# A layer norm's sum of squares: one level of adds on VectorE, the last four partial sums added by four accumulating matmuls

## The chip, the cores and the metric

The kernel runs on one core of a Trainium2 chip. The metric is the time of one execution on the device in microseconds (us). "Before" has three timed runs and one profiled run.

## What is computed

The reference is one inference step of a two-layer decoder trunk: 528 prompt rows (512 and 16 meta rows) and 32 decode rows, 1024 channels wide. Each layer has a sparse attention branch and a short-convolution branch, their gated merge, an output projection, a layer norm, a squared-ReLU MLP and a second layer norm. The change lies in the layer norm alone, which occurs twice per layer:

```python
def _layernorm(x, g, b):
    xf = x.astype(jnp.float32)
    mu = jnp.mean(xf, axis=-1, keepdims=True)
    xc = xf - mu
    var = jnp.mean(jnp.square(xc), axis=-1, keepdims=True)
    y = xc * lax.rsqrt(var + LN_EPS) * g.astype(jnp.float32) + b.astype(jnp.float32)
    return y.astype(x.dtype)
...
    x = _layernorm(ALPHA * x + mix, ln1_g, ln1_b)
    hdn = jnp.square(jax.nn.relu(x @ w_up))
    return _layernorm(ALPHA * x + hdn @ w_down, ln2_g, ln2_b)
```

## The kernel before

Activations are kept transposed: tile X has the 1024 channels as 8 chunks of 128 partitions, and the 560 rows lie along the free axis (R = 560). The engines run hand-written programs that meet at semaphores; the order of each engine's work is the order of the code.

**Matrix products.** fp32 accuracy is made of three products of split numbers: each weight column block (1024 by 128) is loaded by DMA into ST (L321, issued by SyncE), ScalarE casts the high part WH (`high`, L949), GpSimd subtracts to get the low part WL (`rest`, L395), and TensorE runs WH, WL with the activations' high part and WH with their low part (`unit`, L504 for all 560 rows; `half_unit` and `products`, L489, for one half of 280 rows). The activation parts are AXh/AXl and AHh/AHl. ST has two buffers; a buffer is loaded again when GpSimd has read it.

**The layer norm in halves.** The rows are normalised in two halves of 280 (RH). With two layers, two norms per layer and two halves there are eight passes, numbered q = 0 to 7. Even q is the first half of a norm, odd q the second. One pass goes through the engines so:

1. VectorE adds each product column block to X (`residual`, L1782 or L1783) and sums the chunks into XS (`xs_add`, L1774 and L1776).
2. TensorE multiplies XS with the tile `ones`, which holds 1/1024 (`half_mean`, L528): every partition of PSUM tile PB then has the mean.
3. VectorE subtracts it from X (`ln_center`, L1423, two instructions of 4 chunks).
4. ScalarE squares into SQ (`ln_squares`, L975, two instructions of 4 chunks): 8 chunks of 280.
5. VectorE adds the 8 chunks of SQ in three levels, 8 to 4 to 2 (L1430, twice), then 2 to 1 into SS (L1431), and raises `ln_red` (`ln_squares_sum`).
6. TensorE waits for `ln_red` and multiplies SS with `ones` (`half_var`, L534).
7. ScalarE takes the root into SD (`ln_root`, L981), VectorE the reciprocal into RSTD (`ln_inverse`, L1436).
8. VectorE scales X chunk by chunk (L1443), ScalarE adds the shift and writes AXh (L988, L989), VectorE writes AXl (L1447), each chunk raising `a_ready` for the next products.

**What stands around the passes.** In the even passes (q = 0, 2, 4, 6) TensorE runs half products of the output or down projection between the mean and the variance (`out_halves(ph, done, 7, 10)`), and the last two (`10, 12`) behind it; then it starts the products of the next stage, which need `a_ready`. VectorE runs `column_halves`: column half 8's residual and XS add stand right behind `ln_squares_sum`, then those of half 9, then the reciprocal, four scalings, half 10, four more scalings, half 11. ScalarE and GpSimd prepare the next weight blocks in between: ScalarE's cast of one block stands right behind `ln_root`. In the odd passes q = 1, 3, 5 TensorE has products of the next stage for the finished first half on both sides of mean and variance (`up_halves` or `p1_half`). Pass q = 7 stands alone at the end: mean, variance, then the transposes for the output.

Before `ln_squares_sum`'s first add and between its instructions VectorE waits for its own previous instruction (`own.link`).

Of the kernel before, what the change touches and what calls it, by code (L numbers as in the profile page):

```python
# [12 lines left out]
F32 = mybir.dt.float32  # L13
# [5 lines left out]
ALU = mybir.AluOpType  # L19
# [3 lines left out]
P = 128  # L23
# [7 lines left out]
R = RP + RS  # L31
RH = R // 2
# [108 lines left out]
def trunk_program(nc, a):  # L141
    with ExitStack() as ctx:

        def sb(name, shape, dt):
            return ctx.enter_context(nc.sbuf_tensor(name, shape, dt))

        def arena(name, nbytes):

            off = (nc.sbuf_base + 31) // 32 * 32
            sb(name, [P, nbytes // 4], F32)  # L150
            return off

        def at(name, shape, dt, off):
            return nc.alloc_sbuf_tensor_at(name, shape, dt, offset=off)
# [11 lines left out]
        off_q = arena("r_q", BIG)  # L166
        Q = at("Q", [P, KC, R], F32, off_q)
        SD = at("SD", [P, R], F32, off_q)
        RSTD = at("RSTD", [P, R], F32, off_q + 4 * R)
        XS, SS = at("XS", [P, R], F32, off_q + 8 * R), at("SS", [P, R], F32, off_q + 12 * R)  # L170
        off_sg = arena("r_sg", BIG)
        SG = at("SG", [P, KC, R], F32, off_sg)
        QI = at("QI", [P, 4, R], F32, off_sg)
# [51 lines left out]
        SQ = at("SQ", [P, KC, RH], F32, off_m)  # L225
# [7 lines left out]
        ones = sb("ones", [P, P], F32)  # L233
# [18 lines left out]
        PB = ctx.enter_context(nc.psum_tensor("PB", [P, 4, 512], F32))  # L252
# [4 lines left out]
        def sem(name):  # L257
            return ctx.enter_context(nc.semaphore(name))
# [38 lines left out]
        xs_ready, ln_red, ln_hi = sem("xs_ready"), sem("ln_red"), sem("ln_hi")  # L297
        ln_sum, ln_dev, ln_sq, ln_var, ln_sd, ln_norm, ln_aff = (sem("ln_sum"), sem("ln_dev"), sem("ln_sq"),
                                                                sem("ln_var"), sem("ln_sd"), sem("ln_norm"), sem("ln_aff"))
# [183 lines left out]
        def _(pe):  # L483
# [47 lines left out]
            def half_var(q):  # L531
                pe.wait_ge(ln_red, q + 1)
                h = q % 2
                pe.matmul(PB[:, 2 * h + 1, 0:RH], ones[:, :], SS[:, RH * h:RH * h + RH], start=True, stop=True  # L534
                          ).then_inc(ln_var, 1)


            pe.wait_ge(const_in, 16 * (NPG + 7 + 10))
# [12 lines left out]
            for l in range(DEPTH):  # L551
# [11 lines left out]
                for i in range(6):  # L563
                    p1_half(i)
                    if l > 0 and i == 0:
                        half_mean(4 * l - 1)
                    if l > 0 and i == 2:
                        half_var(4 * l - 1)
# [41 lines left out]
                for r in range(1, 5):  # L610
                    c0, n = PTILES[r]
                    for h in range(IH):
# [7 lines left out]
                        for k0 in range(0, KW[r], 512):  # L620
                            k1 = min(k0 + 512, KW[r])
                            for i, (x, y) in enumerate(((QIh[h // 2], KDh), (QIl[:, h // 2], KDh), (QIh[h // 2], KDl))):
                                mm = pe.matmul(PS[j % 2][0:n, k0 // 512, 0:k1 - k0], x[hp, c0:c0 + n], y[hp, k0:k1],  # L623
                                               start=(i == 0), stop=(i == 2))
# [23 lines left out]
                for q in range(4):  # L648
# [6 lines left out]
                    for par in range(2):  # L655
                        for j in range(4):
                            mm = pe.matmul(PS[par][32 * j:32 * j + 32, jh, :],
                                           QS[ID * par:ID * par + ID, 4 * g + j].rearrange("p h s -> p (h s)"),
                                           KIT[j][ID * par:ID * par + ID, :], start=True, stop=True)
# [4 lines left out]
                for b in range(NB):  # L664
                    b4 = 32 * (b % 4)
                    mm = pe.matmul(PB[b4:b4 + 32, 0, 32 * (b // 4):32 * (b // 4) + 32],
                                   QS[0:ID, b].rearrange("p h s -> p (h s)"), KD[0:ID, RP:R], start=True, stop=True)
# [4 lines left out]
                for par in range(2):  # L672
                    for jh in range(2):
                        col = 512 * (2 * par + jh)
                        for g in range(2):
                            pe.matmul(PS[par][0:RS, jh, :], WIB[:, g, :], RELU_S[g][:, col:col + 512],
                                      start=(g == 0), stop=(g == 1))
                for g in range(2):
                    mm = pe.matmul(PB[0:RS, 1, 0:RS], WIB[:, g, :], RELU_S[g][:, PAST:KEYS_S],
                                   start=(g == 0), stop=(g == 1))  # L680
# [12 lines left out]
                for n in range(KVH):  # L693
                    apart(pe, started)
                    with pe.Fori(0, GRP) as i:
                        c = i + GRP * n
# [86 lines left out]
                for g in range(2):  # L783
# [19 lines left out]
                    for q in range(8):  # L803
                        c, n = q // KVH, q % KVH
# [4 lines left out]
                        for b4 in range(4):  # L809
                            mm = pe.matmul(PB[32 * b4:32 * b4 + 32, c, :],  # L810
                                           QP[:, 4 * g + b4, n].rearrange("p h s -> p (h s)"), KTR[b4][:, :],
                                           start=(n == 0), stop=False)
                        mm.then_inc(kt_mm, 1)
                        if n == KVH - 1:
                            if g == 0 and c == 0:
# [3 lines left out]
                                      stop=True).then_inc(ls_mm, 1)  # L819
# [24 lines left out]
                    for c in range(5):  # L844
# [3 lines left out]
                        for j in range(w):  # L848
                            for b4 in range(4):
                                if c in (0, 2) and j == 0:  # L850
# [3 lines left out]
                                mm = pe.matmul(out_s[32 * b4:32 * b4 + 32, :], pt, vv,  # L854
                                               start=(c == 0 and j == 0), stop=(c == 4))
# [36 lines left out]
                half_mean(4 * l)  # L892
                out_halves(WO, l * 24, 7, 10)
                half_var(4 * l)
                out_halves(WO, l * 24, 10, 12)
                up_halves(0, 1)
                half_mean(4 * l + 1)
                up_halves(1, 3)
                half_var(4 * l + 1)
                up_halves(3, 12)  # L900
                for s in range(2):
# [477 lines left out]
        def _(dve):  # L1379
            own = Chain(dve, dve_own, started)  # L1380
# [45 lines left out]
            def ln_squares_sum(q):  # L1426
                h = q % 2
                dve.wait_ge(ln_sq, 2 * q + 2)
                for n in (4, 2):
                    own.link(dve.tensor_tensor(SQ[:, 0:n, :], SQ[:, 0:n, :], SQ[:, n:2 * n, :], ALU.add))  # L1430
                dve.tensor_tensor(SS[:, RH * h:RH * h + RH], SQ[:, 0, :], SQ[:, 1, :], ALU.add).then_inc(ln_red, 1)  # L1431

            def ln_inverse(q):
                rows = slice(RH * (q % 2), RH * (q % 2) + RH)
# [15 lines left out]
            for l in range(DEPTH):  # L1450
# [11 lines left out]
                if l > 0:  # L1462
                    q = 4 * l - 1
                    ln_center(q)
                    ln_squares_sum(q)
                    ln_inverse(q)
                    ln_scale(q, 0, KC)
                    own.link(dve.tensor_scalar(IDX[:, :], IDX[:, :], float(n_rows), None, ALU.add))
                    half_rows().then_inc(idx_ready, 1)
# [51 lines left out]
                for r in range(1, 5):  # L1521
                    c0, n = PTILES[r]
# [15 lines left out]
                for r in range(1, 5):  # L1538
                    n = PTILES[r][1]
# [3 lines left out]
                with own.fori(TOPK_P // 8, 8):  # L1543
                    for r in range(1, 5):
                        n = PTILES[r][1]
                        own.wait(behind=3)
                        own.count(dve.max(top[0:n, r - 1, :], TK[r][0:n, :]))
                    for r in range(1, 5):
                        n = PTILES[r][1]
# [5 lines left out]
                for r in range(1, 5):  # L1555
                    n = PTILES[r][1]
# [161 lines left out]
                for g in range(2):  # L1718
                    for t in range(1, 32, 2):
# [6 lines left out]
                        if t in (11, 19, 27):  # L1726
                            c = (t - 11) // 8
# [75 lines left out]
                def column_halves(group, q, scale, ws):  # L1803
                    for i in range(7):
                        column_half(group, i, scale, ws)
                    ln_center(q)
                    column_half(group, 7, scale, ws)
                    ln_squares_sum(q)
                    column_half(group, 8, scale, ws)
                    column_half(group, 9, scale, ws)  # L1810
                    ln_inverse(q)
                    ln_scale(q, 0, 4)
                    column_half(group, 10, scale, ws)
                    ln_scale(q, 4, KC)
                    column_half(group, 11, scale, ws)
# [14 lines left out]
                ln_center(q)  # L1830
                up_half(0)
                ln_squares_sum(q)
                up_half(1)
                up_half(2)
# [93 lines left out]
```

## Time and profile before

| | |
|---|---|
| Median of 3 runs | 2580.15 us (2579.83 to 2580.17) |
| The profiled execution | 2578.84 us, its span 2577.0 us |
| Mean granted clock of TensorE | 0.941 of full speed |
| TensorE matmuls busy | 2317.9 us, 90% of the span |
| VectorE busy | 1498.2 us, 58% |
| ScalarE busy | 795.6 us, 31% |
| GpSimd busy | 791.7 us, 31% |
| Instructions | 45632 |

The profiled execution took 1.31 us less than the median, and its span, from the first to the last instruction, 1.84 us less than the execution. Busy shares are means over stages of different kinds: where TensorE waits for VectorE in one stage, the 90% says nothing about it. Matmuls are pipelined, so a row's duration is longer than the time until the next can start. An fp32 matmul (L528, L534) shows as two rows, called passes below. A bracket at a row's end is the idle time of the engine before it, and what ended it.

### The profile page before, as it was taken

How to read it: one execution, taken by the hardware profiler on the slowest of the kernel's cores; microseconds unless marked ns; L12 is line 12 of the kernel's file. 1: busy time of each engine (PE TensorE's matmuls, PEld its weight loads, DVE VectorE, ACT ScalarE, POOL GpSimd, SP SyncE). 2: the span in 40 equal slices, each digit the busy share in tenths (PEclk: the TensorE clock that was granted, in tenths of full speed). 3: DMA queues.
4: the chain of work that ended last, by engine and by line, in shares of the span. 5: the costliest groups of instructions: out<-in, count | busy, mean ns of one | idle time of the engine just before them, and what ended most of it. 6: DMA issues, size and time to landing. Idle time of an engine off the chain costs nothing.

```text
span 2577.0 us, 45632 instructions
## 1 busy us (share of the span) xinstructions
PE 2317.9 (90%) x17143; PEld 2129.0 (83%) x17159; DVE 1498.2 (58%) x2234; ACT 795.6 (31%) x1379; POOL 791.7 (31%) x384
## 2 busy tenths in 40 slices
PE   5988999998669999999998889999975899999996
PEld 4965988898339899999998489888953698999995
DVE  3759877779556632132585797777855566132145
ACT  2233343331111432232242443333221125222233
POOL 2410322224213423333542022222331242343440
PEclk9977999999879999999999699999997899999998
DMA  4420222225732312323343022222464232223230
GB/s 117 132 61 10 73 59 59 62 57 184 283 131 65 99 57 83 89 82 90 110 128 88 2 65 56 59 57 57 138 226 193 91 99 73 74 81 88 83 98 35
DMA packets 321366, 238.03 MB, mean 92 GB/s; under 512 B 9560, under 2 KB 309576, under 8 KB 313080
## 3 DMA queue, kind: packets, MB, share of 16 engines
q1 hardware_dynamic: 304424, 154.69, 21.6%
q0 software_dynamic: 12032, 77.07, 7.6%
q10 hardware_dynamic: 4816, 4.96, 0.6%
q8 instruction: 67, 1.10, 0.2%
q14 instruction: 27, 0.22, 0.0%
HBM read 231.73 MB, written 4.96 MB: 92 GB/s over the span
## 4 chain that ended last, share of the span: by engine, by line
PE 78%; DVE 11%; ACT 4%; issue 3%; DMA 2%; ACTq 1%; SPq 0%; DVEq 0%; POOL 0%; POOLq 0%
PE PS L504 54%; PE PS L489 8%; PE PS L797 3%; DVE BB L1690 2%; PE PB L714 2%; PE PS L623 2%; PE PB L738 2%; PE PB L810 1%; DVE SG L1690 1%; PE PS L854 1%; DVE SG L1725 1%; DVE SQ L1430 1%; DMA KVB<-in_cache_v_dram,IDXH 1%; DVE TKS L1575 1%; PE PB L726 1%
## 5 line engine op out<-in xcount | busy, mean ns | idle before, releaser
L395 POOL TENSOR_TENSOR WL<-ST,WH 128x1024 fp32r<-128x1024 f32 x290 | 704.8, 2431 | 1526.1 <-ACT WH L949 1526.0
L949 ACT CAST WH<-ST 128x1024 fp32r<-128x1024 f32 x290 | 303.7, 1047 | 1090.3 <-PE PS L504 943.9
L504 PE MATMUL PS<-AXh,WH 128*128 128x280 f32 x2688 | 575.6, 296 | 21.0 <-DVE AXl L1758 12.6
L504 PE MATMUL PS<-AXl,WH 128*128 128x280 f32 x2688 | 571.6, 294 | 0.0
L504 PE MATMUL PS<-AXh,WL 128*128 128x280 f32 x2688 | 566.4, 292 | 0.0
L504 PEld LDWEIGHTS PS<-AXh,WH 128*128 128x128 f32 x2688 | 432.0, 190 | 23.0 <-issue 21.6
L504 PEld LDWEIGHTS PS<-AXl,WH 128*128 128x128 f32 x2688 | 432.8, 191 | 0.0
L504 PEld LDWEIGHTS PS<-AXh,WL 128*128 128x128 f32 x2688 | 428.1, 190 | 0.0
L504 PE MATMUL PS<-AHh,WH 128*128 128x280 f32 x1152 | 242.0, 291 | 3.6 <-DVE AHl L1823 3.4
L504 PE MATMUL PS<-AHl,WH 128*128 128x280 f32 x1152 | 243.1, 292 | 0.0
L504 PE MATMUL PS<-AHh,WL 128*128 128x280 f32 x1152 | 241.0, 290 | 0.0
L1822 DVE TENSOR_TENSOR MT<-MT 128x560 f32<-128x560 f32 (+1 forms) x76 | 96.3, 1267 | 238.0 <-ACT AHh L1317 217.1
L504 PEld LDWEIGHTS PS<-AHh,WH 128*128 128x128 f32 x1152 | 182.9, 188 | 4.7 <-DVE AHl L1823 3.9
L504 PEld LDWEIGHTS PS<-AHl,WH 128*128 128x128 f32 x1152 | 183.7, 189 | 0.0
L504 PEld LDWEIGHTS PS<-AHh,WL 128*128 128x128 f32 x1152 | 181.6, 188 | 0.0
L797 PEld LDWEIGHTS PS<-ident,KVB 128*128 128x128 f32 x512 | 69.5, 166 | 102.7 <-DVE KTR L1723 42.6
L797 PE MATMUL PS<-ident,KVB 128*128 128x128 f32 x512 | 84.8, 323 | 75.4 <-DVE KTR L1723 39.6
L1782 DVE TENSOR_TENSOR X<-X,PS 128x560 f32 (+2 forms) x60 | 37.2, 621 | 195.7 <-PE PS L504 165.4
L1572 DVE MAX8 top<-TKS 32x8 f32<-32x2080 f32 x64 | 147.3, 2302 | 3.2 <-DVE TKS L1575 2.9
L1575 DVE MATCH_REPLACE8 TKS<-top,TKS 32x2080 f32<-32x2080 f32 x64 | 147.0, 2297 | 0.0
L489 PE MATMUL PS<-AXh,WH 128*128 128x280 f32 x384 | 119.1, 310 | 20.3 <-DVE AXl L1447 11.1
L489 PE MATMUL PS<-AHh,WH 128*128 128x280 f32 x384 | 113.6, 296 | 3.8 <-issue 3.8
(249 smaller groups left out, 3459.1 us busy)
## 6 DMA issues: line engine op xcount, KB each, us to landing
ST<-in_w_in_dram SPq DMA_DIRECT2D x114, 512.0 KB, 3.8
ST<-in_w_up_dram SPq DMA_DIRECT2D x64, 512.0 KB, 4.1
ST<-in_w_down_dram SPq DMA_DIRECT2D x64, 512.0 KB, 3.8
ST<-in_w_conv_out_dram SPq DMA_DIRECT2D x16, 512.0 KB, 3.8
ST<-in_w_attn_out_dram SPq DMA_DIRECT2D x16, 512.0 KB, 3.8
ST<-in_w_o_dram SPq DMA_DIRECT2D x16, 512.0 KB, 3.8
NAT<-in_x_prompt_dram SPq DMA_DIRECT2D x4, 512.0 KB, 3.9
o_y_dram<-NAT ACTq DMA_DIRECT2D x4, 512.0 KB, 2.6
```

The source lines that it names most:

```text
L395: pool.tensor_tensor(WL[slot][:, :, :], ST[s][:, :, :], WH[slot][:, :, :].bitcast(F32), ALU.subtract).then_inc(lo_done[s], 1)
L489: mm = pe.matmul(out, x[:, k, :], y[:, k, r0:r1], start=(k == 0 and y is hi and x is WH[slot]), stop=(k == KC - 1 and y is lo))
L504: mm = pe.matmul(out[:, h, 0:RH], x[:, k, :], y[:, k, RH * h:RH * h + RH], start=(k == 0 and y is hi and x is WH[slot]), stop=(k == KC - 1 ...
L623: mm = pe.matmul(PS[j % 2][0:n, k0 // 512, 0:k1 - k0], x[hp, c0:c0 + n], y[hp, k0:k1], start=(i == 0), stop=(i == 2))
L714: mm = pe.matmul(bank, QST[:, c0:c0 + m], KT[:, n, k0:k1], start=False, stop=True)
L738: mm = pe.matmul(PB[:, 3, 0:m], VN[0:k1, kt, HD * n:HD * n + HD], PPT[i % 2][0:k1, m * kt:m * kt + m], start=(kt == 0), stop=(kt == keys(r ...
L797: tr = pe.transpose(banks[t % 3][:, P * j:P * j + P], KVB[c // 2][b4][:, 4 * (c % 2) + j, HD * n:HD * n + HD], ident[:, :])
L949: act.copy(WH[slot][:, :, :], ST[s][:, :, :]).then_inc(hi_done[s], 1)
L1572: own.link(dve.max(top[0:RS, 0, :], TKS[:, :]), alone=True)
L1575: own.link(dve.match_replace(TKS[:, :], top[0:RS, 0, :], TKS[:, :], NEG_TAKEN), alone=True)
L1690: own.link(dve.reciprocal(v, v))
L1822: own.link(dve.tensor_tensor(h, h, h, ALU.mult))
```

## The change

VectorE does only the first of the three levels of adds, from 8 chunks to 4, and raises `ln_red` there. TensorE multiplies each of the four remaining chunks of SQ with `ones` and accumulates in the same PSUM columns. Tile SS is gone. Nothing else is moved: every other instruction keeps its place in its engine's order.

```diff
-        XS, SS = at("XS", [P, R], F32, off_q + 8 * R), at("SS", [P, R], F32, off_q + 12 * R)
+        XS = at("XS", [P, R], F32, off_q + 8 * R)
...
             def half_var(q):
                 pe.wait_ge(ln_red, q + 1)
                 h = q % 2
-                pe.matmul(PB[:, 2 * h + 1, 0:RH], ones[:, :], SS[:, RH * h:RH * h + RH], start=True, stop=True
-                          ).then_inc(ln_var, 1)
+                for c in range(4):
+                    mm = pe.matmul(PB[:, 2 * h + 1, 0:RH], ones[:, :], SQ[:, c, :], start=(c == 0), stop=(c == 3))
+                mm.then_inc(ln_var, 1)
...
             def ln_squares_sum(q):
                 h = q % 2
                 dve.wait_ge(ln_sq, 2 * q + 2)
-                for n in (4, 2):
-                    own.link(dve.tensor_tensor(SQ[:, 0:n, :], SQ[:, 0:n, :], SQ[:, n:2 * n, :], ALU.add))
-                dve.tensor_tensor(SS[:, RH * h:RH * h + RH], SQ[:, 0, :], SQ[:, 1, :], ALU.add).then_inc(ln_red, 1)
+                dve.tensor_tensor(SQ[:, 0:4, :], SQ[:, 0:4, :], SQ[:, 4:8, :], ALU.add).then_inc(ln_red, 1)
```

## Rows read from the trace of the kernel before

**Rows 1.** Page, the chain that ended last: shares of the span.

```profile
PE 78%; DVE 11%; ACT 4%; issue 3%; DMA 2%; ACTq 1%; SPq 0%; DVEq 0%; POOL 0%; POOLq 0%
```

**Rows 2.** Source view of L1431: duration in ns, least/median/most.

```profile
L1431 DVE TENSOR_TENSOR SS<-SQ x8: 449/450/2607, 872.3 to 2554.4; 128x280 f32<-128x280 f32 x8
```

**Rows 3.** Timeline, TensorE at q = 6: start us, us, engine, line, operation.

```profile
2534.79 0.29 PE L489 MATMUL PS<-AHl,WH 128*128 128x280 f32 x1
2534.91 0.63 PE L534 MATMUL PB<-SS,ones 128*128 128x280 f32 x2
...
2535.52 0.29 PE L489 MATMUL PS<-AHh,WL 128*128 128x280 f32 x1
```

**Rows 4.** Timeline, TensorE at q = 1.

```profile
897.17 0.29 PE L489 MATMUL PS<-AXl,WH 128*128 128x280 f32 x1
897.77 0.74 PE L534 MATMUL PB<-SS,ones 128*128 128x280 f32 x2 [0.31 <-DVE SS L1431]
...
898.47 0.28 PE L489 MATMUL PS<-AXh,WL 128*128 128x280 f32 x1
```

**Rows 5.** Timelines of GpSimd, VectorE and TensorE at q = 0.

```profile
872.46 2.57 POOL L395 TENSOR_TENSOR WL<-ST,WH 128x1024 fp32r<-128x1024 f32 x1 [0.77 <-ACT WH L949]
876.96 2.40 POOL L395 TENSOR_TENSOR WL<-ST,WH 128x1024 fp32r<-128x1024 f32 x1 [1.92 <-ACT WH L949]
...
873.17 2.17 DVE L1774 TENSOR_TENSOR XS<-XS,X 128x280 f32<-128x280 f32 x1
...
878.28 1.39 DVE L1443 SCALAR_TENSOR_TENSOR X<-X,PL,RSTD 128x280 f32<-128x280 f32 x1
...
881.27 0.37 PE L489 MATMUL PS<-AXh,WH 128*128 128x280 f32 x1 [1.53 <-DVE AXl L1447]
```

**Rows 6.** Timelines of VectorE, TensorE, ScalarE, GpSimd and SyncE's queue at q = 2.

```profile
1278.62 2.82 DVE L1430 TENSOR_TENSOR SQ<-SQ 128x560 f32<-128x560 f32 x1
1281.47 2.49 DVE L1431 TENSOR_TENSOR SS<-SQ 128x280 f32<-128x280 f32 x1
...
1284.02 0.74 PE L534 MATMUL PB<-SS,ones 128*128 128x280 f32 x2 [1.84 <-DVE SS L1431]
...
1284.79 0.49 ACT L981 ACTIVATE SD<-PB,eps 128x280 f32<-128x280 f32 x1 [3.81 <-PE PB L534]
1285.18 1.04 ACT L949 CAST WH<-ST 128x1024 fp32r<-128x1024 f32 x1
...
1286.30 2.40 POOL L395 TENSOR_TENSOR WL<-ST,WH 128x1024 fp32r<-128x1024 f32 x1 [2.65 <-ACT WH L949]
...
1287.74 1.27 DVE L1443 SCALAR_TENSOR_TENSOR X<-X,PL,RSTD 128x280 f32<-128x280 f32 x1
...
1280.87 0.37 SPq L321 DMA_DIRECT2D ST<-in_w_in_dram  x1
```

**Rows 7.** Page, DMA issues: KB each, median us from issue to landing.

```profile
ST<-in_w_in_dram SPq DMA_DIRECT2D x114, 512.0 KB, 3.8
ST<-in_w_up_dram SPq DMA_DIRECT2D x64, 512.0 KB, 4.1
```

**Rows 8.** Timelines of SyncE's queue and ScalarE at q = 4.

```profile
2124.59 0.37 SPq L321 DMA_DIRECT2D ST<-in_w_up_dram  x1
...
2128.89 1.04 ACT L949 CAST WH<-ST 128x1024 fp32r<-128x1024 f32 x1
```

**Rows 9.** Timelines of VectorE and TensorE from q = 6's reciprocal to q = 7's sum.

```profile
2536.18 1.91 DVE L1436 RECIPROCAL RSTD<-SD 128x280 f32<-128x280 f32 x1
...
2547.20 1.30 PE L528 MATMUL PB<-XS,ones 128*128 128x280 f32 x2 [5.46 <-DVE XS L1776]
...
2553.65 0.74 DVE L1430 TENSOR_TENSOR SQ<-SQ 128x560 f32<-128x560 f32 x1
...
2554.93 1.30 PE L534 MATMUL PB<-SS,ones 128*128 128x280 f32 x2 [6.43 <-DVE SS L1431]
```

**Rows 10.** Windows, at q = 7: engines' busy us (instructions), then granted clock, DMA, GB/s.

```profile
2555.00:2556.00 1.00, 1.00 (x2) 0.66 (x3) 0.00 (x0) 0.00 (x0) 0.00 (x0) 0.50 0.00 0
```

## The prediction, made before the changed kernel was run

> **What bounds the kernel now.** I read the chain that ended last first: 78% of it is TensorE and 11% VectorE [rows 1]. So work added to TensorE costs its full time unless TensorE waits there anyway, and work taken from VectorE is worth only what TensorE, or the last norm, waits for it. The eight norm passes must therefore be read one by one. The timelines show four kinds.
>
> q = 1, 3, 5: TensorE comes to the variance, waits 0.31 us for the last add by the trace's reckoning, and goes on with products without a break [rows 4]; the other two show the same 0.31. TensorE is the path.
>
> q = 0, 2, 4: the reader is to see two things. TensorE waits after the variance for the first scaled chunks (1.53 us at q = 0), so VectorE is the path [rows 5]. And VectorE itself is held by GpSimd: the XS add at 873.17 takes 2.17 us where 0.45 is usual for 280 columns [rows 2, 5]; GpSimd's subtraction ran from 872.46 to 875.03, and the add ended 0.31 us behind it. Two of the instructions that the change removes are stretched so too: 2.82 and 2.49 us at q = 2 [rows 6].
>
> q = 6: GpSimd has no work left, TensorE does not wait at the variance [rows 3], but the chain behind it does wait: TensorE stands idle 5.46 us until the last XS add releases the next mean [rows 9].
>
> q = 7: everything is in series, at half clock [rows 9, 10].
>
> **The price of a pass.** An fp32 matmul is two passes. At q = 6 the matmul rows before and behind are 2534.79 and 2535.52; without the sum two steps of the usual 0.12 to 0.13 us would lie between them, so the two passes took 0.73 - 0.25 = 0.48 us, 0.24 each [rows 3]. Three more matmuls are six more passes: 1.44 us at full clock. Bounds: 0.23 to 0.30 a pass (at q = 1, after a wait, from 897.77 to 898.47 are 0.70 us with one product in it [rows 4]). I take 0.24, the row where the sum follows other matmuls without a stop, as it will.
>
> **q = 1, 3, 5.** The sum could have started one step behind 897.17, at 897.30; it started at 897.77, and the second product behind it at 898.47, so 1.17 us from 897.30. After the change the first add is long done when TensorE comes: 0.61 us (the same stretch at q = 6, from 2534.91 to 2535.52) and 1.44 = 2.05 us [rows 3, 4]. Each costs 2.05 - 1.17 = 0.88 us; three of them **+2.6 us** (bounds 2.4 to 3.7). The root comes as much later, and so does what ScalarE does behind it; VectorE's two saved adds are worth nothing there.
>
> **q = 0.** TensorE does not wait at the variance and needs 1.44 us more behind it, which its 1.53 us idle ahead of 881.27 just covers [rows 5]. VectorE is rid of two adds, but the add of column half 8 then meets the subtraction that stretched them, and the root is 1.44 us later: by the order of the code the reciprocal comes some 0.7 us earlier, and the first scaling could start at about 877.6. GpSimd's next subtraction lasts from 876.96 to 879.36, and before the change the scaling ended 0.31 us behind that end (878.28 + 1.39 = 879.67). It is stretched to the same end: **0** (bounds -1.6, the 0.7 us and the stretch of 1.39 against 0.50 both gained, and +0.3, if TensorE is late).
>
> **q = 2.** Here TensorE waited 1.84 us for the stretched adds [rows 6]. Now it starts its sum at about 1282.1, and the root stands 0.77 + 1.44 us behind that, at 1284.3 instead of 1284.79. The reciprocal takes 1.9 us and the first scaling can start at about 1286.8. The cast behind the root can move up too, to 1284.7, because its weight tile was asked for at 1280.87 and lands 3.8 us later [rows 6, 7]. With it GpSimd's subtraction moves from 1286.30 to about 1285.8, still ahead of the scaling, and ends 0.5 us earlier; the scaling ends 0.3 us behind it. **-0.5 us** (bounds 0 and -1.8: the reciprocal's lead of 1.0 us, from 1287.74 - 1.9 = 1285.8 to 1284.8, and the stretch of 1.27 against 0.50). The other 1.3 us of TensorE's former wait are late somewhere else: TensorE waits for scaled chunks instead.
>
> **q = 4** is the same, except that the tile asked for at 2124.59 lands after 4.1 us, at 2128.69, against a cast at 2128.89: **-0.2 us** [rows 7, 8] (bounds 0 and -1.8, as at q = 2).
>
> **q = 6.** The root comes 1.44 us later, and the reciprocal at 2536.18, which stood right behind it, too; scaling, halves 10 and 11 and the XS add follow in line up to the mean that TensorE waits for [rows 9]: **+1.4 us** (bounds 1.3 to 1.8).
>
> **q = 7.** The second add (0.74) and the last (0.45) with the steps between go: TensorE starts when the second add did, at about 2553.67 instead of 2554.93, 1.26 us earlier [rows 2, 9]. The six passes run at the granted clock of 0.50, the 1.2 GHz level [rows 10]: 0.24 at 2.4 GHz is 0.47 there, 2.8 us. **+1.5 us** (bounds +0.2 and +1.6).
>
> **The sum:** 2.6 + 0 - 0.5 - 0.2 + 1.4 + 1.5 = +4.8 us. The profiled execution took 2578.84 us and would take 2583.6; the median of the runs is 1.31 us above it, so I forecast 2580.15 + 4.8 = **2585.0 us**, 0.19% more. A measurement of this kernel can tell about 0.2%, 5.2 us: a forecast just inside "no difference". That tile SS goes costs and moves nothing.
>
> **Who inherits the stretch.** The rows say that a stretched instruction ends when GpSimd's does, so taking the stretched one away hands the stretch to the next of its kind, here the XS add of column half 8 and later the first scaling [rows 5]. The Trainium skill, "SBUF — State Buffer", section "Who interferes with whom", has this as a rule: a VectorE instruction with two SBUF inputs and a GpSimd instruction that reads SBUF exclude each other for the whole instruction, whichever starts first. By it the gains at q = 0, 2, 4 stay as small as in my sum; reading the stretch as the adds' own gives the "faster" rival below. The trace agrees with the rule in the XS add's 2.17 us.
>
> **Rivals.**
>
> *Slower: GpSimd takes the lead away at q = 2 and 4 too.* If the cast cannot start earlier than before, because the tile lands later than 4.3 us after its request (1280.87 to 1285.18), the subtraction holds the first scaling until the old time, as I already expect at q = 0. The two gains are 0 and the sum is +5.5 us: **2585.7 us**, slower. For it: 4.1 is the median of one of the two kinds of tile [rows 7], and 0.2 us decide. Against: at 1285.18 the cast followed the root at once, with no wait for the tile. Chance 0.30. A dearer pass adds to that side: at 0.30 us the three odd passes cost 1.1 us more, q = 6 0.4: 2586.5 us, chance 0.06.
>
> *The adds' stretch is freed, not handed on.* If at q = 0, 2, 4 the first scaling gets in before GpSimd, the reciprocal's lead (0.7 us, and 1.0 twice) and the stretch (1.39 and, twice, 1.27 against 0.50) both reach the path, 2.7 + 2.4 = 5.1 us: 5.5 - 5.1 = +0.4, **2580.6 us**. Against: the scaling would have to start 0.6 to 1 us earlier than I work out. Chance 0.11.
>
> *The clock rises in the last sum.* If TensorE were granted full clock within q = 7's longer sum, the six passes would cost 1.44 instead of 2.8 us, and the total be **2583.6 us**. Against: the clock is 0.50 there, after 6.43 us idle [rows 9, 10]. Chance 0.08. The Trainium skill, "TensorE: Matmul & The Clock Gate", Part 1, has the rule behind it: the throttled state is the default and activity releases it. The trace shows the fall and no rise here.
>
> *Faster: the stretched adds were the path themselves.* Then q = 2 and 4 gain the whole 2.82 + 2.49 = 5.3 us each in place of 0.5 and 0.2, and the sum is 4.8 + 0.7 - 10.6 = -5.1 us: **2575.0 us**. For it: at q = 2 they are what VectorE does while TensorE waits [rows 6]. Against: GpSimd's subtractions are not moved, and TensorE needs its half products first. Chance 0.03. That the change fails to do what it says is not in sight: two VectorE instructions per pass are gone and six passes added, in place.
>
> **How the numbers follow.** My forecast has 0.42; with the freed stretch (0.11) and the clock (0.08) it makes 0.61 for no difference. Slower has 0.30 + 0.06 = 0.36, faster 0.03. The predicted time is the likeliest case. The range goes from the freed stretch, 2580.6, to the dearer pass with both gains lost, 5.5 + 1.1 + 0.4 = +7.0: 2587.1 us.
>
> **What would show it.** Right: L1430 has 8 instructions, not 16, and SS is gone; L534's sum has eight rows a pass of the norm; at q = 1 TensorE has no idle before the sum, and the products behind it come 0.9 us later; at q = 0 the first scaling still ends just behind a GpSimd subtraction; at q = 2 and 4 the wait at the variance is gone and the waits behind it have grown; from q = 6's sum to q = 7's mean the chain is 1.4 us longer. Wrong: passes 0.3 us apart, first scalings of 0.5 us at q = 0, 2, 4, or a granted clock of 1 in q = 7.

## The result, and the profile after

The changed kernel took 2588.14 us (median of 6 runs, 2585.8 to 2591.96) against 2579.99 us for the kernel before on the same chip (6 runs, 2574.57 to 2580.72): ratio 1.0038, 95% interval 1.0025 to 1.0051. It is slower, by more than forecast: 2585.0 us was said, with 2587.1 as the upper end. Two further series of it (below) gave 1.0025 each. All 27 runs together have a mean of 2586.1 us, 7.9 us above that of the 129 runs of the kernel before that were made beside all the kernels told of here (95% interval 6.5 to 9.2 us). The forecast was +4.8. The first six runs came out long: their mean is 2588.8 us, that of the 21 later ones 2585.3, so part of the first +8.1 us belongs to that one series and did not come again.

The profiled execution took 2591.96 us, its span 2590.2 us. On its page, the line of the engines' busy times and the chain that ended last:

```profile
PE 2332.5 (90%) x17207; PEld 2139.4 (83%) x17207; DVE 1484.4 (57%) x2218; ACT 794.6 (31%) x1379; POOL 790.9 (31%) x384
...
PE 80%; DVE 9%; ACT 4%; issue 3%; DMA 2%; ACTq 1%; SPq 0%; POOL 0%; DVEq 0%; POOLq 0%
```

VectorE's busy time fell by 13.8 us and TensorE's rose by 14.6; the chain moved two points from VectorE to TensorE [rows 1]. The source views of the sum (L535) and of the one add that is left (L1430), with duration in ns, least/median/most, show that the change does what it says:

```profile
L535 PE MATMUL PB<-SQ,ones x64: 397/399/836, 873.5 to 2568.7; 128*128 128x280 f32 x64
...
L1430 DVE TENSOR_TENSOR SQ<-SQ x8: 1324/1325/1327, 868.8 to 2563.9; 128x1120 f32<-128x1120 f32 x8
```

All eight adds now last the same 1.32 us. None is stretched, where the last level of before went up to 2.6 us [rows 2].

**q = 1.** TensorE's timeline (start us, us, engine, line, operation), where [rows 4] had an idle of 0.31 us:

```profile
898.74 0.29 PE L489 MATMUL PS<-AXl,WH 128*128 128x280 f32 x1
898.87 2.05 PE L535 MATMUL PB<-SQ,ones 128*128 128x280 f32 x8
900.55 0.50 PE L489 MATMUL PS<-AXh,WH 128*128 128x280 f32 x1
900.89 0.29 PE L489 MATMUL PS<-AXh,WL 128*128 128x280 f32 x1
```

The idle is gone, and the second product behind the sum stands 2.02 us after the sum's start (forecast 2.05).

**q = 0.** GpSimd, VectorE and TensorE, which answer to [rows 5]; a bracket is the idle time before the row:

```profile
869.71 2.67 POOL L395 TENSOR_TENSOR WL<-ST,WH 128x1024 fp32r<-128x1024 f32 x1 [2.13 <-ACT WH L950]
872.85 2.37 POOL L395 TENSOR_TENSOR WL<-ST,WH 128x1024 fp32r<-128x1024 f32 x1 [0.47 <-ACT WH L950]
877.65 2.40 POOL L395 TENSOR_TENSOR WL<-ST,WH 128x1024 fp32r<-128x1024 f32 x1 [2.44 <-ACT WH L950]
...
871.14 1.54 DVE L1773 TENSOR_TENSOR XS<-XS,X 128x280 f32<-128x280 f32 x1
874.30 1.23 DVE L1773 TENSOR_TENSOR XS<-XS,X 128x280 f32<-128x280 f32 x1
876.23 1.91 DVE L1435 RECIPROCAL RSTD<-SD 128x280 f32<-128x280 f32 x1 [0.70 <-ACT SD L982]
878.17 2.19 DVE L1442 SCALAR_TENSOR_TENSOR X<-X,PL,RSTD 128x280 f32<-128x280 f32 x1
...
881.97 0.37 PE L489 MATMUL PS<-AXh,WH 128*128 128x280 f32 x1 [0.19 <-DVE AXl L1446]
```

Two XS adds and the first scaling carry the stretch, and each ends 0.30 or 0.31 us behind one of GpSimd's three subtractions. The scaling ends at 880.36, 0.31 us behind GpSimd's 880.05, as before. TensorE's idle ahead of the first new product fell from 1.53 to 0.19 us: the longer sum filled it.

**q = 2**, TensorE, ScalarE, GpSimd, VectorE, which answer to [rows 6]:

```profile
1284.41 2.05 PE L535 MATMUL PB<-SQ,ones 128*128 128x280 f32 x8
...
1286.50 0.49 ACT L982 ACTIVATE SD<-PB,eps 128x280 f32<-128x280 f32 x1 [3.28 <-PE PB L535]
1286.99 1.05 ACT L950 CAST WH<-ST 128x1024 fp32r<-128x1024 f32 x1
...
1288.11 2.39 POOL L395 TENSOR_TENSOR WL<-ST,WH 128x1024 fp32r<-128x1024 f32 x1 [2.33 <-ACT WH L950]
...
1289.04 1.77 DVE L1442 SCALAR_TENSOR_TENSOR X<-X,PL,RSTD 128x280 f32<-128x280 f32 x1
```

Counted from each trace's own mean at q = 2 (1272.26 before, 1274.66 after), the sum starts 2.01 us earlier, the root 0.69 us earlier, and the first scaling ends 0.60 us earlier, again 0.31 us behind GpSimd.

**q = 6 and 7**, TensorE (as [rows 9]):

```profile
2558.79 1.30 PE L528 MATMUL PB<-XS,ones 128*128 128x280 f32 x2 [5.46 <-DVE XS L1775]
2565.26 4.10 PE L535 MATMUL PB<-SQ,ones 128*128 128x280 f32 x8 [5.17 <-DVE SQ L1430]
2569.16 1.17 PE L941 MATMUL PS<-ident,X 128*128 128x128 f32 x8
```

and the window of the last sum, with the columns of [rows 10]:

```profile
2565.26:2569.36 4.10, 4.10 (x9) 2.96 (x10) 0.00 (x0) 0.00 (x0) 0.00 (x0) 0.50 0.00 0
```

The last sum begins 1.26 us earlier behind its mean (6.47 for 7.73 us), and it takes 4.10 us for 1.30. The granted clock is 0.50 throughout, the 1.2 GHz level.

Where the time lies is best read between the marks that each trace has: the starts of the means, numbered 0 to 7, and the first key transpose of layer 1 (KT1). In us, one traced execution each:

| stretch | before | null | changed | again | again2 | forecast change |
|---|---|---|---|---|---|---|
| mean 0 to 1 (q=0) | 27.37 | 27.50 | 27.39 | 27.50 | 27.40 | 0 |
| mean 1 to 2 (q=1) | 381.78 | 381.72 | 383.48 | 382.54 | 382.62 | +0.88 |
| mean 2 to 3 (q=2) | 27.57 | 27.57 | 26.98 | 27.02 | 27.15 | -0.5 |
| mean 3 to KT1 (q=3) | 104.62 | 104.61 | 105.83 | 105.12 | 105.23 | +0.88 |
| KT1 to mean 4 | 711.40 | 711.38 | 717.89 | 714.75 | 714.86 | 0 |
| mean 4 to 5 (q=4) | 27.69 | 27.59 | 27.49 | 27.51 | 27.34 | -0.2 |
| mean 5 to 6 (q=5) | 381.62 | 381.59 | 382.49 | 383.56 | 383.64 | +0.88 |
| mean 6 to 7 (q=6) | 22.04 | 22.03 | 23.45 | 23.45 | 23.45 | +1.4 |
| mean 7 to end (q=7) | 29.82 | 29.82 | 31.37 | 31.36 | 31.36 | +1.5 |

("null", "again" and "again2" are the runs of the next section.) Five of the passes are as forecast. The odd ones are not: they scatter from +0.5 to +2.0 us. And a stretch that the change does not touch, KT1 to mean 4, is longer in all three traces of the changed kernel, by 3.4 to 6.5 us. How far a single trace of that stretch can be trusted is seen in "tail" (next section), which is the kernel before up to q = 6: 708.02 us there, 3.4 less than before.

### The profile page after: what moved, and what is told of

It reads as the page before. It is cut to its first block, busy times and chain, and to the rows that moved or that the text cites. A ratio compares the mean times of both kernels' runs of the same rounds, so it can differ in the third digit from the quotient of the medians.

```text
span 2590.2 us, 45728 instructions
## 1 busy us (share of the span) xinstructions
PE 2332.5 (90%) x17207; PEld 2139.4 (83%) x17207; DVE 1484.4 (57%) x2218; ACT 794.6 (31%) x1379; POOL 790.9 (31%) x384
## 4 chain that ended last, share of the span: by engine, by line
PE 80%; DVE 9%; ACT 4%; issue 3%; DMA 2%; ACTq 1%; SPq 0%; POOL 0%; DVEq 0%; POOLq 0%
PE PS L504 54%; PE PS L489 10%; PE PS L798 3%; DVE BB L1689 2%; PE PB L715 2%; PE PB L739 2%; PE PS L624 2%; PE PB L811 1%; DMA KVB<-in_cache_v_dram,IDXH 1%; DVE SG L1689 1%; PE PS L855 1%; DVE SG L1724 1%; DVE X L1442 1%; DVE TKS L1574 1%; PE PB L727 1%
```

## The experiments

### The three kinds of pass by themselves

A list of passes says where the four matmuls stand; the rest is as in the kernel before. This is "odd"; the list is (0, 2, 4) in "even" and (6, 7) in "tail".

```diff
+FOUR = (1, 3, 5)
...
+                if q in FOUR:
+                    for c in range(4):
+                        mm = pe.matmul(PB[:, 2 * h + 1, 0:RH], ones[:, :], SQ[:, c, :], start=(c == 0), stop=(c == 3))
+                    mm.then_inc(ln_var, 1)
+                else:
...
+                if q in FOUR:
+                    dve.tensor_tensor(SQ[:, 0:4, :], SQ[:, 0:4, :], SQ[:, 4:8, :], ALU.add).then_inc(ln_red, 1)
+                    return
```

The changed kernel once more ("again"):

> The changed kernel once more. Theory A (the sum place by place is whole, +4.8 us, and the rest of the measured +8.1 us was the chance of where the clock's half-speed windows fell): some 4.8 to 6 us slower than before, and the trace shows the same steps at the passes (0, +0.9, -0.5, +0.9, -0.2, +0.9, +1.4, +1.5) with other half-clock stretches in the second layer's attention. Theory B (the change itself makes TensorE's half-clock stretches longer, at the passes or in the attention behind them): 8 to 11 us slower again, and the half-clock time again about 20 us above that of before.

Four matmuls at q = 1, 3, 5 only ("odd"):

> Four matmuls at q = 1, 3, 5 alone, the other passes as before. Theory A: +2.6 us (0.88 us each). Theory B, if a shift of the second layer against the first is what lengthens its attention: +2.6 and another 3 to 6 us, since q = 1 and 3 lie ahead of it.

At q = 0, 2, 4 only ("even"):

> Four matmuls at q = 0, 2, 4 alone. Theory A: 0 - 0.5 - 0.2 = -0.7 us. Theory B, if moving TensorE's idle time from the variance to the wait for scaled chunks keeps the clock down longer: +1 to +3 us, with longer half-clock stretches right behind q = 0, 2, 4 and slower products around the next mean.

At q = 6 and 7 only ("tail"):

> Four matmuls at q = 6 and 7 alone. Both theories: +1.4 + 1.5 = +2.9 us, since nothing lies behind them that the clock could lengthen; the trace up to q = 6 is that of before but for where the half-clock windows fall, and so shows how much that alone moves.

Measured, against 33 runs of the kernel before on the same chip (median 2577.83 us, 2569.76 to 2585.89):

| kernel | median us (runs) | ratio, 95% interval | difference of means, us |
|---|---|---|---|
| again | 2585.08 (11) | 1.0025 [1.0015, 1.0034] | +7.0 |
| odd | 2584.55 (11) | 1.0020 [1.0007, 1.0032] | +5.6 |
| even | 2578.33 (11) | 0.9998 [0.9989, 1.0007] | +0.1 |
| tail | 2579.55 (11) | 1.0009 [1.0000, 1.0019] | +1.8 |

The parts add up to the whole (+7.5 against +7.0). The even passes are worth nothing, the tail costs some 2 us, and the odd passes cost twice the 2.6 us of the forecast. The trace of "odd" says the same: its three stretches are longer by 0.8, 2.0 and 2.2 us (382.57, 106.65 and 383.78), 5.0 together. "again" lies between theory A's 4.8 to 6 us and theory B's 8 to 11. "odd" has the size of theory B but not its way: its attention stage in layer 1 is no longer than before (91.8 us, see below).

At q = 5 the reason can be read. The windows begin at the mean and end at the second product behind the sum; columns are length, busy time (instructions) of PE, PEld, DVE, ACT and POOL, granted clock, DMA share, GB/s. The kernel before:

```profile
2143.54:2146.54 3.00, 3.00 (x23) 2.91 (x23) 2.30 (x2) 1.79 (x3) 1.93 (x1) 0.99 0.00 0
2146.54:2151.35 4.81, 4.50 (x33) 4.18 (x32) 4.30 (x8) 2.91 (x6) 0.00 (x0) 1.00 0.38 109
```

and "again":

```profile
2144.90:2147.90 3.00, 3.00 (x14) 2.74 (x14) 1.82 (x2) 1.31 (x3) 1.91 (x1) 0.58 0.03 6
2147.90:2154.71 6.81, 6.81 (x49) 6.44 (x47) 4.55 (x8) 3.50 (x6) 0.00 (x0) 1.00 0.27 77
```

In the first 3 us TensorE does 23 matmuls at a granted clock of 0.99, or 14 at 0.58: half clock lasts for 2.5 us behind the mean. The stretch from mean to second product is 9.81 us instead of 7.81. Over the changed odd passes of "changed", "again", "again2" and "odd" it goes from 8.62 us, where no half clock falls in, to 10.14 with 3.23 us of it, some 0.47 us for each us of half clock.

In the kernel before, half clock costs less, but not nothing. Up to some 0.9 us of it costs as much there: 7.81 us with 0.05 us of half clock, 8.11 with 0.67, 8.23 with 0.90 (q = 3 of "even"), and the idle of 0.30 or 0.31 us is still there. The mean itself is slower, so VectorE's first subtraction, and with it the adds, comes later. Beyond that the slower products use the idle up. q = 1 of "shift2" (told of below, the kernel before up to this pass) has 2.90 us of half clock behind its mean at 893.44. These are VectorE's subtractions there and TensorE's sum, which has no idle ahead of it:

```profile
894.62 2.55 DVE L1426 TENSOR_TENSOR X<-X,PB 128x1120 f32<-128x1120 f32 x2 [1.49 <-PE PB L528]
901.42 0.64 PE L534 MATMUL PB<-SS,ones 128*128 128x280 f32 x2
...
902.02 0.29 PE L489 MATMUL PS<-AXh,WL 128*128 128x280 f32 x1
```

and the same in "odd" at q = 5, with 2.99 us of half clock behind its mean at 2148.75:

```profile
2149.93 2.55 DVE L1429 TENSOR_TENSOR X<-X,PB 128x1120 f32<-128x1120 f32 x2 [1.49 <-PE PB L529]
2156.77 2.05 PE L537 MATMUL PB<-SQ,ones 128*128 128x280 f32 x8
...
2158.79 0.29 PE L490 MATMUL PS<-AXh,WL 128*128 128x280 f32 x1
```

The subtractions begin 1.18 us behind the mean in both (0.70 at q = 5 of the kernel before), and the sums start at nearly the same place, 7.98 and 8.02 us. With no wait to set against the longer sum, the pass takes 8.58 us with one matmul and 10.04 with four, 1.46 more: the whole price of three matmuls, which the forecast put at 1.44.

### Odd passes with the clock kept up, and with two sums

To take the half clock out, unused products were put into the first half product behind q = 0, 2 and 4, where TensorE waits for scaled chunks. Nobody reads what they write.

```diff
+WARM = {2: 8, 4: 14}
...
+                    if warm:
+                        for _ in range(WARM.get(k, 0)):
+                            pe.matmul(PB[:, 3, 0:RH], WH[slot][:, 0, :], hi[:, 0, 0:RH], start=True, stop=True)
...
```

Put into the changed kernel ("after_warm") and into the kernel before ("before_warm", and again "before_warm2"):

> The changed kernel, and 8 and 14 products without use, into PSUM columns that nobody reads, ahead of the third and the fifth chunk of the first half product after q = 0, 2 and 4, where TensorE waits for scaled chunks. Theory C (an odd pass costs 0.85 us, and 0.24 us more for each us that TensorE stands at half clock between its mean and its sum, since the wait for the adds that hid this is gone): no half-clock time at q = 1, 3, 5, the second product behind the sum 8.60 us after the mean in each of them, some 0.5 to 1.5 us less in all than the changed kernel. Rival (half clock there is chance and has nothing to do with the idle time at q = 0, 2, 4): the half-clock time at the odd passes stays and so does the time.

> The kernel before with the same unused products. Theory C: the sum's cushion hid most of the half clock, so the second product behind the sum comes 7.78 us after the mean in each odd pass, against 7.81 to 8.11; the mean itself comes 0.3 to 0.5 us earlier at q = 1, 3, 5; 1 to 2 us less than before in all, which the spread of the runs may hide. Rival: no change.

> The unused products in the kernel before, once more: the first measurement gave +4.0 us, where its own steps in the passes add up to -0.6 us and the rest of its trace was longer ahead of the first pass. If that was chance: -1 to +1 us now. If unused products do cost something in the whole: +3 to +5 us again.

The other two keep a second level of adds at q = 1, 3, 5 and sum two chunks there ("two_odd"). "best", with its repeat "best2", adds to that the unused products and four chunks at q = 2 and 4, and sums one chunk at q = 0, 6 and 7: its list is (1, 2, 4, 2, 4, 2, 1, 1). This is "two_odd":

```diff
+SUMS = (1, 2, 1, 2, 1, 2, 1, 1)
...
+                n = SUMS[q]
+                for c in range(n):
+                    mm = pe.matmul(PB[:, 2 * h + 1, 0:RH], ones[:, :], SQ[:, c, :] if n > 1 else SS[:, RH * h:RH * h + RH],
+                                   start=(c == 0), stop=(c == n - 1))
+                mm.then_inc(ln_var, 1)
...
+                    e = dve.tensor_tensor(SQ[:, 0:n, :], SQ[:, 0:n, :], SQ[:, n:2 * n, :], ALU.add)
+                    if n == SUMS[q]:
+                        e.then_inc(ln_red, 1)
+                        return
+                    own.link(e)
```

> The kernel before, with two levels of adds and two matmuls at q = 1, 3, 5 alone. If the price of the odd passes is the passes on TensorE less the wait for the adds: the sum is released 0.48 us earlier, just when TensorE comes, and has two passes more (0.47 us), so the second product behind the sum comes 7.70 to 7.80 us after the mean at full clock: 0 us. If the matmuls cost more than their passes (more weight loads, a switch each time): +0.3 us or more for each odd pass.

> Four matmuls at q = 2 and 4, two at q = 1, 3, 5, one (as before) at q = 0, 6 and 7, and the unused products. By the steps measured so far: -0.55 and -0.2 at q = 2 and 4, 0 at the odd passes, 1 to 2 us less from the clock: 2 to 3 us under before. If the unused products bring nothing: -0.7 us, not to be told from no change.

> The mixed version once more (four matmuls at q = 2 and 4, two at q = 1, 3, 5, one elsewhere, and the unused products). By its steps -1.3 us; the first measurement gave -1.3. If before is 0.2% or more above it: a version that beats both. If it lies within 2 us of before: no difference that can be told.

Measured:

| kernel | median us (runs) | ratio, 95% interval | difference of means, us |
|---|---|---|---|
| after_warm | 2584.52 (11) | 1.0023 [1.0014, 1.0033] | +5.6 |
| before_warm | 2581.58 (12) | 1.0012 [1.0003, 1.0021] | +4.0 |
| before_warm2 | 2582.95 (11) | 1.0007 [0.9997, 1.0016] | +3.3 |
| two_odd | 2578.90 (12) | 1.0002 [0.9990, 1.0014] | +0.2 |
| best | 2578.39 (11) | 0.9992 [0.9980, 1.0004] | -1.3 |
| best2 | 2577.33 (12) | 0.9996 [0.9986, 1.0006] | -0.8 |

In all five traces with the unused products no half clock falls between mean and sum in any of the 15 odd passes, where in the 13 other traces it does in 35 of 39. So it comes from TensorE's idle time in the even passes ahead of them: filled, it leaves no half clock behind. With the clock up, a changed odd pass has one price. TensorE at q = 3 of "after_warm":

```profile
1302.68 2.05 PE L541 MATMUL PB<-SQ,ones 128*128 128x280 f32 x8
1304.36 0.50 PE L491 MATMUL PS<-AXh,WH 128*128 128x280 f32 x1
1304.70 0.29 PE L491 MATMUL PS<-AXh,WL 128*128 128x280 f32 x1
```

The window from its mean to the second product behind the sum:

```profile
1295.95:1304.69 8.74, 8.74 (x59) 8.29 (x60) 3.88 (x3) 3.27 (x5) 2.19 (x1) 1.00 0.23 62
```

In "before_warm" the sum waits for the adds as in [rows 4]:

```profile
1310.76 0.74 PE L541 MATMUL PB<-SS,ones 128*128 128x280 f32 x2 [0.29 <-DVE SS L1443]
```

and its window is

```profile
1303.58:1311.47 7.89, 7.60 (x53) 7.19 (x54) 5.08 (x5) 3.27 (x5) 2.19 (x1) 1.00 0.26 67
```

8.74 against 7.89 us at q = 3, 8.72 against 7.89 at q = 1 and 5: **0.83 to 0.85 us** is the price of the pass, and the forecast's 0.88 was right at full clock. What it left out is the half clock. The whole times are less clean. "after_warm" is 2.2 us faster than the 27 runs of the changed kernel (95% interval 0.4 to 4.1), where theory C expected 0.5 to 1.5. By its passes "after_warm" should lie 4.6 us above "before_warm" (2.5 for the odd ones, 2.7 at q = 6 and 7, 0.6 less at q = 2 and 4); it lies 1.9 above the mean of the two. Both traces of "before_warm" take 31.6 and 32.1 us from mean 7 to the end instead of 29.8, in a wait for the output that comes back below. The unused products do not pay as a repair either: they cost the kernel before 3 to 4 us, where theory C expected 1 to 2 us less. Two sums cost nothing in these passes at full clock. In "best", TensorE goes through without a stop:

```profile
1304.81 0.29 PE L491 MATMUL PS<-AXl,WH 128*128 128x280 f32 x1
1304.94 1.19 PE L541 MATMUL PB<-SQ,ones 128*128 128x280 f32 x4
1305.76 0.50 PE L491 MATMUL PS<-AXh,WH 128*128 128x280 f32 x1
1306.10 0.29 PE L491 MATMUL PS<-AXh,WL 128*128 128x280 f32 x1
```

The second product behind the sum comes 7.87 us after the mean there. At half clock two sums do cost: 8.88 us at q = 1 of "two_odd" with 2.36 us of it, against 8.28 with 2.10 and one sum at q = 1 of "even". "best" is some 9 us faster than the changed kernel, but against the kernel before its interval holds 1 both times; the 2 to 3 us less that were expected did not show.

### The kernel before as if it were a change, and the changed kernel a third time

> The kernel before, unchanged, run as if it were a change. If the runs' spread of about 3 us is chance from run to run, its mean is that of before within 2 us and its trace differs from the first one only where half-clock windows fall. If the offsets stay with a session or a place on the chip, it can be off by several us, and then so can the other comparisons, beyond their intervals.

> The changed kernel a third time. By the steps (0.0, 0.85 and clock, -0.55, 0.85 and clock, -0.2, 0.85 and clock, 1.4, 1.55; some 5.5 us with the clock) 4.5 to 7 us slower. If something else of the change costs (the first two measurements gave 8 and 7 us), 7 to 8 us once more, and the trace shows where.

"null" gave 2579.99 us (11 runs), ratio 1.0009 [0.9996, 1.0022]; "again2" 2585.03 us (10 runs), 1.0025 [1.0015, 1.0034]. The 129 runs of the kernel before have a mean of 2578.2 us and a standard deviation of 3.2, from 2564.6 to 2585.9. The three runs that the forecast started from, within 0.34 us of each other, showed none of this.

### A later start for layer 1's attention

From the last score product to the first mask product (PB<-MP,identb) of layer 1 no instruction is changed. Windows over that stage (columns as above) in the kernel before:

```profile
1450.27:1542.25 91.98, 76.21 (x553) 64.47 (x551) 89.05 (x214) 41.42 (x57) 18.97 (x8) 0.90 0.15 40
```

and in the changed kernel:

```profile
1453.36:1547.70 94.34, 78.65 (x553) 65.98 (x551) 90.48 (x216) 41.46 (x57) 18.96 (x8) 0.87 0.15 39
```

The same 553 matmuls at a mean granted clock of 0.87 instead of 0.90 take 2.4 us longer. "again" had 94.07 us and "again2" 93.94; "null", "tail", "even", "odd" and "two_odd" had 91.8 to 92.2; but "before_warm" too had 94.6, and the same stage of layer 0, which lies ahead of every edit, took 94.3 us in the kernel before and 92.2 in "null", the same program. So the longer stage is not the changed kernel's alone. Over both layers of all 18 traces, the length of the stage rises by 0.37 us for each us of half clock in it (correlation 0.99). To ask whether the later start does this, eight unused products were put ahead of a product of layer 1 behind q = 3 in the kernel before ("shift"), fourteen in the changed kernel ("again_shift"), each twice.

```diff
                 for i in range(6, 12):
+                    if l > 0 and i == 8:
+                        for _ in range(8):
+                            pe.matmul(PB[:, 3, 0:RH], WH[P1_SLOT[3]][:, 0, :], AXh[:, 0, RH:R], start=True, stop=True)
                     p1_half(i)
```

> The kernel before with eight unused products (0.125 us each at full clock, results read by nobody) put into the first product of layer 1 behind q=3, where TensorE is never idle, so that everything behind starts 1.0 us later; no norm is touched. Theory D (a later start of layer 1's attention puts more of its time at half clock): the stage from the last score product to the first mask product in layer 1 takes 93.5 to 94.5 us instead of 92.0, with 23 to 24 us of half clock in it instead of 17.5, and the median lies 2.5 to 3.5 us above before. Rival (chance from run to run): the stage stays at 92, the time is +1.0 us.

> The same kernel as shift, a second time, for a second trace and twice the runs: theory D expects the stage at 93.5 to 94.5 us again and +2.5 to +3.5 us, the rival 92 us or a different length in the two traces, and +1.0 us.

> The changed kernel with fourteen unused products (1.75 us) at the same place. Theory D: the stage in layer 1 falls back from 94 to 92 us, which pays for the products, and the time is no more than that of the changed kernel, some +5.5 to +7.5 us over before. Rival (chance): the stage as often at 94 as in the changed kernel, and the time +1.75 us over the changed kernel's +7.7, so +9.5 over before.

> The same kernel as again_shift, a second time: theory D expects the stage at 92 us in both traces and no more time than the changed kernel; the rival a stage that differs between the traces, and +9.5 us over before.

| kernel | median us (runs) | ratio, 95% interval | difference of means, us | stage, us |
|---|---|---|---|---|
| shift | 2579.83 (12) | 1.0008 [0.9997, 1.0018] | +1.5 | 94.31 |
| shift2 | 2581.78 (11) | 1.0012 [1.0000, 1.0024] | +3.3 | 92.15 |
| again_shift | 2590.03 (6) | 1.0045 [1.0033, 1.0057] | +11.7 | 92.22 |
| again_shift2 | 2587.94 (5) | 1.0033 [1.0020, 1.0046] | +8.3 | 89.83 |

The differences are against the mean of all 129 runs of the kernel before. Of the four stage lengths two came out as theory D expected (94.31 and 92.22); "again_shift2" lost the 94 too, but fell to 89.83 and not to 92. "shift2" missed: its untouched q = 1 had met 2.9 us of half clock (382.37 us from mean 1 to 2 instead of 381.7), and so had q = 3, so its stage began later than the eight products alone would have it; that this made the miss is argued, not shown. The times tell less. "shift" and "shift2" together are 2.3 us above the kernel before (95% interval 0.6 to 4.0), which holds the rival's 1.0 as well as D's 2.5 to 3.5. The changed kernel is no faster for the shorter stage; its 10.2 us over the kernel before (both series, 95% interval 7.9 to 12.4) fit the rival's +9.5 and not D's +5.5 to +7.5. In the trace of "again_shift" what the stage gave is lost elsewhere: at q = 5 the stretch from mean 5 to 6 is 383.81 us, and at the end ScalarE waits longer for an output's DMA, which the change does not touch either:

```profile
2585.82 1.01 ACT L1368 COPY NAT<-PS 128x1024 f32<-128x1024 f32 x1 [3.37 <-DMA o_y_dram<-NAT]
```

In the changed kernel's own trace that wait is

```profile
2585.05 1.01 ACT L1365 COPY NAT<-PS 128x1024 f32<-128x1024 f32 x1 [1.05 <-DMA o_y_dram<-NAT]
```

So the stage's length follows the half clock in it, and moving its start can change that. Counted from the program's start, no place decides it: the stage begins at 1448.48 us in "again" and takes 94, and at 1448.42 in "even" and takes 92. That it adds 2 us to the changed kernel's time is not shown.

## Why the prediction was wrong, point by point

**The odd passes are the step that failed.** "Each costs 2.05 - 1.17 = 0.88 us; three of them +2.6 us (bounds 2.4 to 3.7)". The mechanism holds at full clock: TensorE is the path there, its idle is gone, and the price is 0.83 to 0.85 us. What failed is that the sum took two things as fixed and gave no reason for them: that TensorE has full clock in these passes, and that the wait inside the 1.17 us is always there to be set against the longer sum. (The trace of before had 0.41 and 0.67 us of half clock behind the means of q = 1 and 3, which [rows 4] does not show.) The wait was also a cushion. Where TensorE is at half clock for 2.9 us behind the mean, the slower products use it up, and the same three matmuls cost 1.46 us. The half clock itself also fell otherwise. At q = 5, of the six traces with four matmuls there and no products for the clock, five show 2.5 to 3.0 us of it between mean and sum, and of the seven such traces with one or two sums none more than 0.3. At q = 1 and 3 there is no such difference (1.1 us on average with four matmuls, 1.2 with one or two). The three traces of the changed kernel give +1.1, +0.8 and +1.6 us at q = 1, 3 and 5 on average, 3.5 instead of 2.6, which the forecast's bounds still hold; "odd" was 5.6 us slower (95% interval 3.6 to 7.6), which they do not. The half clock comes from TensorE's idle time in the even passes; why so much of it reaches q = 5 with four matmuls was not found.

**q = 0** was right: the traces differ by less than 0.15 us. The stretch was handed on to the XS adds and the first scaling, as the prediction said under "Who inherits the stretch". At q = 0 and at q = 2 the scaling ends 0.31 us behind GpSimd's subtraction. The Trainium skill, "SBUF — State Buffer", section "Who interferes with whom", has a VectorE instruction with two SBUF inputs contend with a GpSimd instruction that reads SBUF, under an exclusive lock; the trace agrees.

**q = 2** gained 0.5 us by the table's stretches (forecast 0.5) and **q = 4** 0.2 (0.2). The rival in which GpSimd takes this lead away is refuted at q = 2: the cast moved up with the root. The "freed stretch" and the "faster" rival are refuted by scalings of 2.19 and 1.77 us, and by "even", which is as fast as the kernel before.

**q = 6** was right to 0.01 us (+1.41), **q = 7** too (+1.54). The clock did not rise in the last sum: 0.50 in the window. For "tail" the difference of means, +1.8 us, lies below the 2.9 of the traces, inside its interval of 0 to about 4.9.

**The sum.** The three traces give 3.5 + 0 - 0.5 - 0.2 + 1.4 + 1.5 = +5.7 us by their passes, 0.9 us over the forecast; the 27 runs give 7.9, with 6.5 as the lower end. The 2 us longer attention stage of the same three traces would fill the rest, but the shifted kernels did not bear that out, so this part stays open. Forecast from a mean of 2578.2 instead of three runs' 2580.15, the time would have been 2583.0; the mean of the 27 runs is 2586.1. That mean lies inside the stated range, which ends at 2587.1; the 2588.14 of the first six runs does not. The agreement of those three runs showed nothing of the kernel's spread of some 3 us, which the range should have held.

## What to carry to other kernels

Idle time on the bounding engine just ahead of a wait is not only what the next step could start earlier: it also hides slower products ahead of it, until they have used it up. Before filling it, see in a window what clock the products in front of it get. Where two engines meet, move just so much work that neither waits: at full clock, one level of adds less was free where two cost 0.84 us a pass. And take the spread of a kernel from many runs before setting a range of a few us.

## What the runs showed of the hardware

- The same four matmuls of a sum: 2.05 us for their eight rows at q = 1, at full clock, and 4.10 us at q = 7, at the 1.2 GHz level.
- Half clock outlasts the idle time that it comes from. Unused products in TensorE's idle time at q = 0, 2 and 4 took it out of all 15 odd passes behind (granted clock 1.00); without them it reached up to 3.2 us into a pass of unbroken products.
- An engine that the profile shows as busy throughout need not have the full clock. In the first 3 us behind q = 5's mean TensorE is shown busy for 3.00 of 3.00 us at 0.99 in the kernel before and at 0.58 in "again". The Trainium skill, "TensorE: Matmul & The Clock Gate", Part 1, says that the throttled state is the default and activity releases it; the rows show half clock lasting on into a stretch of unbroken products.
- Placement of half clock is worth as much as a small edit. The untouched attention stage of layer 1 took 89.8, 92 or 94 us with 12, 18 or 23 to 24 us of half clock in it, and the untouched stage of layer 0 took 92 or 94 us in traces of the same program.
